# A layer step with forgetting attention and sparse attention: the order of the first two column groups of the input projection is swapped

## The reference

```
h  = rmsnorm(x, norm1_g)                 # 1024 prompt rows and 32 sample rows, width 1024
z  = h @ w_in                            # 2848 columns, float32
q_fox, k_fox, v_fox = z[:, 0:512], z[:, 512:1024], z[:, 1024:1536]
f, q_nsa, nsa, win, gates = the other columns
fox_kv = stack([k_fox, v_fox])           # an output of the step, and an input of the attention
# then: forgetting attention, sparse attention with three branches, output projection,
# gated feed-forward with a causal convolution, residuals, final norm
```

## Time and profile before

| what | value |
|---|---|
| median of 3 runs | 2197.22 us (2197.01 to 2201.42) |
| the profiled execution, its own time | 2202.11 us |
| its span from first to last instruction | 2200.4 us |
| TensorE (PE) busy | 1897.6 us, 86% of the span |
| VectorE (DVE) busy | 996.6 us, 45% |
| ScalarE (ACT) busy | 732.0 us, 33% |
| GpSimd (POOL) busy | 575.9 us, 26% |
| mean DMA traffic | 104 GB/s |

### The profile page before, as it was taken

How to read it: one execution, slowest core, us unless ns; L and a number is a source line. 1 busy time by engine, 2 the same in 40 slices (tenths; PEclk the granted TensorE clock), 3 DMA queues, 4 the chain that set the end, 5 groups by cost and what they waited for, 6 DMA issues and landing times. The chain is left out here.

```text
span 2200.4 us, 32229 instructions
## 1 busy us (share of the span) xinstructions
PE 1897.6 (86%) x11816; PEld 1668.6 (76%) x11816; DVE 996.6 (45%) x1897; ACT 732.0 (33%) x1456; POOL 575.9 (26%) x684
## 2 busy tenths in 40 slices
PE   3998899996574568999999969899999999979995
PEld 2887677995342267888888858699999999966674
DVE  2323411422231235777777755233233332366897
ACT  2323311311121113777777743121111211133352
POOL 4310212334243312222221130112122121143452
PEclk9899999997886756999999989999999999999998
DMA  5443532436846392323320032211111111054543
GB/s 138 90 105 139 212 123 98 154 110 191 275 157 211 96 168 62 73 63 75 67 58 15 1 147 86 67 39 48 48 38 57 38 48 48 29 194 153 182 138 128
DMA packets 169576, 229.27 MB, mean 104 GB/s; under 512 B 44684, under 2 KB 112709, under 8 KB 169319
## 3 DMA queue, kind: packets, MB, share of 16 engines
q1 hardware_dynamic: 141690, 146.09, 21.8%
q0 software_dynamic: 27760, 81.55, 13.2%
HBM read 192.62 MB, written 40.18 MB: 106 GB/s over the span
## 5 line engine op out<-in xcount | busy, mean ns | idle before, releaser
L2251 DVE TENSOR_TENSOR pa_probs_T_lo<-pa_t,pa_probs_T_hi 128x512 fp32r<-128x512 f32 (+3 forms) x288 | 147.5, 533 | 64.9 <-ACT pa_probs_T_hi L2192 64.0
L121 PE MATMUL gate_acc<-o_T_hi,w_gate_split_hi 128*128 128x352 f32 x528 | 171.3, 324 | 2.0 <-ACTq L2630 2.0
L121 PE MATMUL up_acc<-o_T_hi,w_up_split_hi 128*128 128x352 f32 x528 | 171.1, 324 | 0.7 <-DVEq L2673 0.7
L122 PE MATMUL gate_acc<-o_T_lo,w_gate_split_hi 128*128 128x352 f32 x528 | 170.0, 322 | 0.0
L122 PE MATMUL up_acc<-o_T_lo,w_up_split_hi 128*128 128x352 f32 x528 | 169.9, 322 | 0.0
L123 PE MATMUL gate_acc<-o_T_hi,w_gate_split_lo 128*128 128x352 f32 x528 | 169.8, 322 | 0.0
L123 PE MATMUL up_acc<-o_T_hi,w_up_split_lo 128*128 128x352 f32 x528 | 169.8, 322 | 0.0
L2192 ACT ACTIVATE pa_probs_T_hi<-pa_t 128x512 fp32r<-128x512 f32 (+3 forms) x288 | 131.7, 472 | 90.9 <-PE pa_t L2117 87.6
L2117 PE MATMUL pa_t<-ident,pa_scores 128*128 128x128 f32 x816 | 138.6, 276 | 17.8 <-DVE pa_probs_T_lo L2251 17.8
L2177 ACT ACTIVATE pa_scores<-pa_scores,pa_neg_max 128x128 f32<-128x128 f32 (+1 forms) x192 | 143.3, 746 | 30.7 <-DVE pa_neg_max L2215 26.7
L121 PE MATMUL y_acc<-w_down_split_hi,act_split_hi 128*128 128x512 f32 x308 | 125.0, 406 | 20.2 <-DVE act_split_lo L2995 19.7
(11 more groups left out here) (442 smaller groups left out, 4785.6 us busy)
## 6 DMA issues: line engine op xcount, KB each, us to landing
w_down_raw<-in_w_down SPq DMA_DIRECT2D x59, 512.0 KB, 4.5
fox_k_pages<-in_cache_fox_kv SPq DMA_DIRECT2D x64, 256.0 KB, 9.7
w_rows<-in_cache_fox_kv POOLq DMA_DIRECT2D x64, 256.0 KB, 6.3
w_gate<-in_w_gu SPq DMA_DIRECT2D x22, 512.0 KB, 3.8
w_up<-in_w_gu SPq DMA_DIRECT2D x22, 512.0 KB, 3.8
w_rows<-in_w_in SPq DMA_DIRECT2D x5, 2048.0 KB, 8.7
sel_pages<-in_cache_nsa_kv POOLq DMA_DIRECT2D x64, 128.0 KB, 7.4
pa_k_fox<-scratch_kf_d POOLq DMA_DIRECT2D x32, 256.0 KB, 6.2
```

The source lines that it names most:

```text
L121: pe.matmul(out, a[0][at], b[0][bt], start=start, stop=False)
L122: pe.matmul(out, a[0][at], b[1][bt], start=False, stop=False)
L2251: dve.tensor_tensor(lo, PT[n % 2][:, 0:m * P].rearrange("p (m n) -> p m n", n=P), hi, ALU.subtract).then_inc(s_cd, 1)
```

## The change

The list of groups begins with the forget values, and the two loads of weights that are written outside the list are swapped with it. The group that is multiplied while the rows are still being normalised has then no transposes, no key copies and no key stores; all of these fall into the second group.

```
@@ front, SyncE
-            sp.dma_start(c.wr[0][:, :, :], d["w_in"][0].rearrange("(k p) n -> p k n", p=P)[:, :, C_KF:C_KF + 512]).then_inc(c.s_wr[0], 16)
+            sp.dma_start(c.wr[0][:, :, :], d["w_in"][0].rearrange("(k p) n -> p k n", p=P)[:, :, C_VF:C_VF + 512]).then_inc(c.s_wr[0], 16)
@@
-CHUNKS_IN = [("k_fox", C_KF, 512), ("v_fox", C_VF, 512), ("nsa", C_NSA, 512), ("win", C_WIN, 288), ("q_fox", C_QF, 512), ("q_nsa", C_QN, 512)]
+CHUNKS_IN = [("v_fox", C_VF, 512), ("k_fox", C_KF, 512), ("nsa", C_NSA, 512), ("win", C_WIN, 288), ("q_fox", C_QF, 512), ("q_nsa", C_QN, 512)]
@@ project, SyncE
-            sp.dma_start(w[1][:, :, :], w_in[:, :, C_VF:C_VF + 512]).then_inc(s_w[1], 16)
+            sp.dma_start(w[1][:, :, :], w_in[:, :, C_KF:C_KF + 512]).then_inc(s_w[1], 16)
```

## The result

The swapped kernel takes 2188.27 us (median of 5 runs, 2184.94 to 2188.61), the kernel before 2198.24 us beside it (5 runs, 2197.01 to 2201.42). The ratio is 0.9948, with a 95% interval of 0.9933 to 0.9962: 0.5% faster. (The ratio is taken between the means of the runs; the two medians alone would give 0.9955.) Forecast were 2186 us, with 2183 to 2189 for the case that came about and up to 2192 over all cases.

What follows compares the result with a forecast made beforehand. TensorE, busy 86% of the span, bounds the kernel, with one hole in the projection. Terms -9.51 - 1.57 - 0.2 + 0 = -11.3 us take 2197.2 to 2185.9, predicted as 2186; range 2183 to 2189, to 2192 over all cases.

Steps and rivals of the forecast that it cites:

- the case that came about: First case: TensorE's hole in the projection closes and nothing takes its place, 2185.9 us; chance 0.65.
- The hole: First group, before block 7's turn: TensorE's idle 9.51 us, from a key copy waiting for a key store, goes.
- the clock behind it: TensorE just after the idle stretch: the lower clock, 3.35 us against 1.78 for the same instructions, goes, saving 1.57 us.
- The move of the transposes: Nine forget-key turns move from first to second group: 0.43 us saved and 0.41 added each, about -0.2 us.
- The key copies and stores in the second group: VectorE's copies and 16 stores of 256 KB move there; cost 0, up to 3 us if two loads fall together.
- The z store: First group: step 2's store lands about 246, before ScalarE's step 5 copy needs it; cost 0, at most 5.1 us.
- second rival: In the first group the z store takes the key store's place as the wait, priced 4.6 us: 2190.5; chance 0.12.
- The third group's weights: Landed at 262.2, wanted about 271 behind the second group's first z copy: stay hidden, 9 us to spare, cost 0.
- The rest of the program: Stages after the projection start from a barrier, so the whole gain was let through.
- The third rival: The hole was smaller in the runs than in the profiled execution: 2190.8 us, a gain of 6.4; chance 0.12.
- The fourth: Rival of no change: the 11 us are given back in the stage behind the projection, 2197 us; chance 0.07.
- The fifth: Rival: key stores in the second group stop TensorE, making it slower, 2202 us or more; chance 0.04.

Runs made afterwards that it cites:

- second try without block 1's stores: Kernel before without block 1's key stores at their time; block 5's copies stored to block 1's place too, at block 5's turn; 2192.29 us, one run.

## Why the prediction was right

**The hole, -9.51 us, and the clock behind it, -1.57 us.** Right: the hole is 9.44 to 9.58 us in all three profiles of before, and none is left after. The step that rested on the least, that the copy's large packets hold the key store, is shown by two edits that leave all stores in place: the copy later, or in small packets, and the hole is gone. The Trainium skill, DMA: Bandwidth & Descriptors, Queues, rings and completion order, says that a DMA engine takes one packet of each queue in turn; the runs agree, with 21.9 us for a store between packets of 65 KB and 6.6 us between packets of 2 KB.

One reading on the way to the hole was off, without harm to the sum. The prediction lets block 3's key copy start at 240.4, when VectorE had finished the work before. But a key copy also waits for TensorE to turn its block; the one of block 2 shows it:

```profile
236.05 0.69 DVE L898 CAST kt_hi<-z_tp 128x512 fp32r<-128x512 f32 x1 [2.53 <-PE z_tp L745]
```

A step of 6.89 us later, at 242.9, block 3's was due, so the store held it for 10.6 us and not for 13.2. The price was read from TensorE's own idle time, 9.51 us, which leaves 1.1 us of VectorE's delay covered.

**The move of the transposes, -0.2 us.** Too small to be seen: 0.43 us per turn were to be saved and 0.41 added. The periods came out as 6.44 and 6.00 us, so by the same subtraction 0.45 us saved (6.89 - 6.44) and 0.45 added (6.00 - 5.55), and no run shows the -0.2 us. The sum of the three terms was -11.3 us; the means of the projection are 297.4 (three profiles) and 286.1 (two), a difference of 11.3. The two profiles of the swapped kernel differ by 0.6 us, so the agreement to 0.1 is chance.

**The key copies and stores in the second group, 0.** Right, with little to spare for VectorE. The longest key store there took 8.4 us, beside the fifth group's weights, where 9 were free: it landed at 298.6, and the key copy that needed its buffer started at 299.8. No key copy waited for one.

**The z store, 0.** Right, and the nearest to going wrong. The stores of step 2 and step 3 both came 1.4 us before ScalarE wanted them. With two stores more in the queue the second rival came about, at 6 us in the projection, more than the 4.6 us at which it was priced.

**The third group's weights, 0.** They landed at 257.4 (226.93 and 30.5 us) and were wanted at 270.4: 13 us to spare, where 9 were forecast.

**The rest of the program, 0.** The third rival fell: the hole is no shorter in faster runs (9.44 us in the run of 2194.5 us, 9.51 in that of 2202.11). The fourth fell: behind the projection nothing is given back, with 239.4 us of sample attention after and 239.0 to 243.9 before, and a rest of 1433.9 and 1435.7 us after and 1432.7 to 1435.1 before. The fifth had no wait to start from. The time measured is 2.3 us above the forecast. 1.0 us of this is the kernel before, 2198.24 with the later runs where 2197.22 was shown. The rest is inside the interval: 11.3 us are a ratio of 0.9949, and 0.9948 was measured. What makes the runs of one kernel differ by 4 to 8 us is shown in part: the sample attention had lengths from 237.2 to 246.7 us, the start of the projection moved by up to 2.7 us. Why they do stays open.

## What to carry to other kernels

A long copy of large contiguous rows from memory to memory is cheap for the queue that issues it and dear for every small store on the same DMA engines: here a store had to wait for five packets of 65 KB of some 2.6 us each, 13 us by that count, and stores issued in the first half of the copy took 16 to 22 us to land. Before reordering work around such a wait, look at what shares the engines; moving the copy, cutting it into runs of 2 KB, or taking the store off the path gave the same 0.5% here, and the first and the last together gave no more.

When a wait is taken away, compute for the next one in the same stretch when it is due and when it is met. Here 1.4 us were left, and two more stores would have cost half the gain.

## What the runs showed that was not expected

A short hole cost more clock than a long one. In the second try without block 1's stores TensorE was idle for 3.57 us. The busy time by stretch shows the hole and the clock at 0.50 up to 266, six us after work had begun again:

```profile
256.75:260.30 3.55, 0.01 (x1) 0.00 (x0) 3.21 (x5) 0.69 (x2) 2.04 (x3) 0.88 0.70 261
260.00:262.00 2.00, 1.68 (x11) 1.62 (x12) 0.27 (x1) 0.58 (x2) 0.11 (x1) 0.50 0.87 326
262.00:264.00 2.00, 2.00 (x7) 1.61 (x7) 1.50 (x3) 2.00 (x3) 0.00 (x0) 0.50 0.50 193
264.00:266.00 2.00, 2.00 (x6) 1.58 (x5) 2.00 (x3) 1.58 (x2) 1.83 (x3) 0.50 0.30 90
266.00:268.00 2.00, 2.00 (x9) 1.60 (x8) 2.00 (x3) 0.00 (x0) 1.15 (x2) 0.94 0.88 236
```

From the turn of block 8 to the eleventh matmul of the product behind it there were 6.1 us (260.32 to 266.39), and 3.4 us in the kernel with the copy in small packets, which has no hole: 2.6 us lost at 1.2 GHz, where the hole of 9.5 us lost 1.57. The clock inside the holes tells why: it is 0.88 in this one and 0.63 in the long one. So the long hole had most of its time at the lower level behind it, while nothing ran, and here nearly all of it fell on work. The cost of a hole is its length plus 1.6 to 2.6 us here: 11.1 us for the long one and 6.2 for this, so a hole shorter by 5.9 us saved 4.9.

And the copy in 2 KB runs was not free, only paid for where nothing waited. Its two parts took SyncE's queue 7.47 us, and the load of weights behind them 13.83 us, where it had been 0.82 us and 0.40. These weights landed 38.8 us after the copy's issue (226.14 to 264.94), with 34.7 before (227.52 to 262.2). They were wanted at 273.3, 8 us later still; with less room the small packets would have cost time of their own.
